# A recurrent scan's small products: values and updates stacked for contractions over 128 rows

## The chip, the cores and the metric

The kernel runs on one core of one Trainium2 chip. The metric is the device time of one execution in microseconds. The kernel is one long program, a two-part network of which the part looked at here takes about 8%.

## The reference

The reference is a network of attention, convolution, MLP and recurrent mixers. The change touches one recurrent mixer, RWKV7, over 256 context and 512 latent tokens, 8 heads of 64 channels, once forwards and once backwards:

```python
def _rwkv7_scan(S0, r, w, k, v, kk, a):
    def step(S, inp):
        r_t, w_t, k_t, v_t, kk_t, a_t = inp
        sa = jnp.einsum('bhvk,bhk->bhv', S, kk_t)
        S = (S * w_t[:, :, None, :] - sa[..., None] * (kk_t * a_t)[:, :, None, :]
             + v_t[..., None] * k_t[:, :, None, :])
        return S, jnp.einsum('bhvk,bhk->bhv', S, r_t)
    xs = tuple(jnp.swapaxes(t, 0, 1) for t in (r, w, k, v, kk, a))
    S, ys = lax.scan(step, S0, xs)
    return jnp.swapaxes(ys, 0, 1), S
...
    yf_c, Sf_c = _rwkv7_scan(S0, r_c, wf_c, k_c, v_c, kk_c, a_c)
    yb_c, Sb_c = _rwkv7_scan(S0, *_flip_seq(r_c, wb_c, k_c, v_c, kk_c, a_c))
    yf_l, _ = _rwkv7_scan(Sf_c, r_l, wf_l, k_l, v_l, kk_l, a_l)
    yb_l, _ = _rwkv7_scan(Sb_c, *_flip_seq(r_l, wb_l, k_l, v_l, kk_l, a_l))
```

Per token and head, the state S is decayed, corrected by a rank-one update (u, from S and kk) and by another (from v and k), and read by r.

## The kernel before

`rwkv_scan` (L3022 to L3332) works in chunks of 64 tokens: 12 turns (4 of context, 8 of latents) for each of two directions. A direction is an object `t` (a `Dir`) with four PSUM banks `a`, `b`, `c`, `d`. The 8 heads lie as 4 pairs q; of a pair, head h=0 has partitions 0 to 63 and head h=1 partitions 64 to 127 (`HALVES`). Almost every product is 64 rows by 64 columns by 64, in one quarter of TensorE's array: which rows and which columns follows from the partition half of the operands and of the output. The generator `heads` yields the eight (q, h).

A turn's steps are, by name, on three engines (list `order`, L3081):

- `cross` and `join` (PE) multiply decayed keys, values' keys and queries into scores of 64 x 64 and 64 x 128, which DVE (`start`, `mask`) takes to SBUF. `turn` (PE) transposes keys, `token_major` (ACT) copies them.
- `apply`, `keep`, `grow_by`, `merge` for l = 1 to 5 invert a triangular matrix by doubling: `apply` multiplies (into `d`), `keep` (DVE, L3318 and L3319) copies the wanted part into `yl[l]` under a mask, `grow_by` multiplies it into `c` and `d`, `merge` (ACT, L3259, L3262) copies the result. After l = 5 it is `solution`.
- In `apply` of the turn after, the tail of the turn before is done: l = 1 makes g = scores x v + kr x state (into `c`), `g` (ACT, L3265) copies it; l = 2 makes u = solution x g, and also starts the state's bank `a` with keys x v and the output's bank `b` with v x scores; `u` (ACT, L3268) copies u.
- `push` (PE) adds keys x u to `a` and state x queries to `b`; `state` (DVE, L3323, L3326) adds `a` to the state and decays it; `apply` with l = 3 adds u x scores to `b`, and `y` (ACT, L3271) copies `b` out. `apply` with l = 3 also turns the values of the turn to come token-major (product with an identity), `v` (ACT, L3251) copies them into `v_tok`.

So u lies on the *other* half of the partitions than its head's v, since `solution` x g is written across.

Each engine runs this list in its own program order, fully unrolled; forwards and backwards alternate, the backward direction half a list (`lag`) behind. The list is the same before and after. An engine that waits for a semaphore holds all that comes behind it in its queue. There is no DMA in the loop but that of the program's own code.

Below, a half-turn is the work between `apply` 2 of one direction and `apply` 2 of the other: one direction's second half of the list and the other's first half. There are 24 of them. In each PE goes through: apply 2 F, apply 4 B, grow_by 4 B, join B, grow_by 2 F, apply 5 B, push F, grow_by 5 B, apply 3 F, turn B, apply 1 B, grow_by 3 F, grow_by 1 B, cross F (F and B for the directions, which change places in the next).

All PE products of the loop but `turn` are recorded at L3115, the helper `one`; `turn` at L3229.

Of the kernel before, what the change touches and what calls it, by code (L numbers as in the profile page):

```python
# [13 lines left out]
ACT = mybir.ActivationFunctionType  # L14
# [3007 lines left out]
def rwkv_scan(kit, f, cum, kk, b_neg, y_out, decays, small, spare):  # L3022
# [27 lines left out]
        t.first, t.zx = take(2, 4), take(2, 4)  # L3050
        t.kb_tok = [take(2, 4) for _ in range(2)]
    for d, t in enumerate(dirs):
        t.v_tok = [take(4) for _ in range(2)]
        t.yl = [None] + [take(4) for _ in range(5)]
        t.solution, t.grow, t.state, t.g0, t.u = (take(4) for _ in range(5))
        t.fwd = d == 0
        t.decay = decays[:, d]
        t.own = t.decay[:, :, 1:65] if t.fwd else t.decay[:, :, 0:64]
        t.before = t.decay[:, :, 0:64] if t.fwd else t.decay[:, :, 1:65]
        t.bearer, t.first_bearer = small[:, d:d + 1], small[:, 2 + d:3 + d]  # L3060
        t.ends = [small[:, 4 + 12 * d + 4 * e:8 + 12 * d + 4 * e] for e in range(3)]
        t.seen = kit.const("seen_fwd" if t.fwd else "seen_back")
        t.merge = [kit.const(f"merge{l}")[:, 64 * d:64 * d + P].rearrange("p (m n) -> p m n", m=2).bitcast(mybir.dt.uint32)
                   for l in range(6)]
        t.cum, t.y = cum[d], y_out[d]
        t.a, t.b, t.c, t.d = (ps[:, 4 * d + n, :].rearrange("p (m q n) -> p m q n", m=2, q=4) for n in range(4))
        t.ab, t.cd = ps[:, 4 * d:4 * d + 2, :], ps[:, 4 * d + 2:4 * d + 4, :]
        t.prefilled, t.emptied = ph.sem("scan_prefilled"), ph.sem("scan_emptied")
        t.grown, t.bent, t.rest_bent = ph.sem("scan_grown"), ph.sem("scan_bent"), ph.sem("scan_rest_bent")
        t.crossed, t.joined, t.started, t.masked = (  # L3070
            ph.sem(f"scan_{s}") for s in ("crossed", "joined", "started", "masked"))
        t.turned, t.token_major, t.v_turned, t.v_copied = (
            ph.sem(f"scan_{s}") for s in ("turned", "token_major", "v_turned", "v_copied"))
        t.applied, t.kept, t.grown_by, t.merged = (
            [None] + [ph.sem(f"scan_{s}{l}") for l in range(1, 6)] for s in ("applied", "kept", "grown_by", "merged"))
        t.gathered, t.g_copied, t.solved, t.u_copied = (
            ph.sem(f"scan_{s}") for s in ("gathered", "g_copied", "solved", "u_copied"))
        t.state_made, t.added, t.decayed, t.out_made, t.y_copied = (
            ph.sem(f"scan_{s}") for s in ("state_made", "added", "decayed", "out_made", "y_copied"))
# [29 lines left out]
    with ph as block:  # L3109
        @block.tensor  # L3110
        def _(pe):
# [14 lines left out]
                    pe.wait_ge(sem, turn + 1)  # L3126

            def apply(t, l, i):
                level, tail, front = there(i), there(i - 1), there(i + 1)
                x = t.first[:, 1] if l == 1 else t.zx[:, 1]  # L3130
                scored = t.scored[i % 2]
                old, new = (i - 1) % 2, (i + 1) % 2
                old_scored = t.scored[old]
                if level and l == 1:
                    pe.wait_ge(t.started, i + 1)
                    pe.wait_ge(t.masked, i + 1)
                if level and l > 1:
                    pe.wait_ge(t.merged[l - 1], i + 1)
                if tail and l == 1:
                    pe.wait_ge(t.token_major, i)  # L3140
                    pe.wait_ge(t.v_copied, i)
                    pe.wait_ge(t.merged[5], i)
                if tail and l == 2:
                    pe.wait_ge(t.g_copied, i)
                    done(i, t.token_major)
                    if not level:
                        done(i - 2, t.added)
                        done(i - 2, t.y_copied)
                for q, h, half, other in heads():
                    if level:  # L3150
                        mm = one(t.d[half, 1, q, :], scored[other, h, q, 0:64], x[other, q, :])
                        if (q, h) == (3, 1):
                            mm.then_inc(t.applied[l], 1)
                    if tail and l == 1:
                        one(t.c[half, 1, q, :], old_scored[half, h, q, 0:64], t.v_tok[old][half, q, :], start=q == 0)
                    if tail and l == 2:
                        one(t.a[half, 0, q, :], t.kb_tok[old][half, h, q, :], t.v_tok[old][half, q, :], start=q == 0)
                    if front and l == 3:
                        at = offset(t, i + 1) + 1
                        mm = one(t.c[half, 1, q, :], f[half, RW_V + q, at:at + 64], same[half, :])  # L3160
                        if (q, h) == (3, 1):
                            mm.then_inc(t.v_turned, 1)
                if tail and l == 1:
                    done(i - 2, t.decayed)
                    if i == 1:
                        pe.wait_ge(t.emptied, 1)
                    for q, h, half, _ in heads():
                        mm = one(t.c[half, 1, q, :], t.kr[old][half, q, 0:64], t.state[half, q, :], start=False)
                    mm.then_inc(t.gathered, 1)
                if tail and l == 2:  # L3170
                    for q, h, half, other in heads():
                        mm = one(t.c[other, 1, q, :], t.solution[half, q, :], t.g0[half, q, :])
                        if (q, h) == (3, 1):
                            mm.then_inc(t.solved, 1)
                        one(t.b[half, 0, q, :], t.v_tok[old][half, q, :], old_scored[half, h, q, 64:P], start=q == 0)
                if tail and l == 3:
                    pe.wait_ge(t.state_made, i)
                    for q, h, half, other in heads():
                        mm = one(t.b[half, 0, q, :], t.u[other, q, :], old_scored[other, h, q, 64:P], start=False)
                    mm.then_inc(t.out_made, 1)  # L3180

            def grow_by(t, l, i):
                if l == 1:
# [1 line left out]
                if l == 2:  # L3185
                    done(i - 1, t.u_copied)
                if l == 3:
                    done(i + 1, t.v_copied)
                if there(i):
                    z = t.first[:, 0] if l == 1 else t.zx[:, 0]  # L3190
                    pe.wait_ge(t.kept[l], i + 1)
                    for q, h, half, other in heads():
                        mm = one(t.c[half, 0, q, :], t.yl[l][half, q, :], z[half, q, :])
                        if l < 5:
                            mm = one(t.d[other, 0, q, :], z[half, q, :], t.yl[l][half, q, :])
                    mm.then_inc(t.grown_by[l], 1)

            def step(t, name, l, i):
# [4 lines left out]
                elif name == "push" and there(i - 1):  # L3203
                    old = (i - 1) % 2
                    pe.wait_ge(t.u_copied, i)
                    for q, h, half, other in heads():
                        one(t.b[half, 0, q, :], t.state[half, q, :], t.kr[old][half, q, 64:P], start=False)
                        mm = one(t.a[half, 0, q, :], t.kb_tok[old][other, h, q, :], t.u[other, q, :], start=False)
                    mm.then_inc(t.state_made, 1)
                elif name == "cross" and there(i + 1):  # L3210
                    kr = t.kr[(i + 1) % 2]
                    pe.wait_ge(t.bent, i + 2)
# [22 lines left out]
        def _(act):  # L3235
            def step(t, name, l, i):
                if name == "grow" and there(i + 1):
# [7 lines left out]
                    else:  # L3245
                        act.activation(t.grow[:, :, 1:64], t.cum[:, :, at:at + 63], ACT.Exp, scale=DECAY)
                    act.activation(t.ends[(i + 1) % 3].unsqueeze(2), t.cum[:, :, at + 63:at + 64],
                                   ACT.Exp, scale=DECAY).then_inc(t.grown, 1)
                elif name == "v" and there(i + 1):
                    act.wait_ge(t.v_turned, i + 2)  # L3250
                    act.activation(t.v_tok[(i + 1) % 2], t.c[:, 1], ACT.Copy).then_inc(t.v_copied, 1)  # L3251
                elif name == "token_major" and there(i + 1):
                    act.wait_ge(t.turned, i + 2)
                    act.activation(t.kb_tok[(i + 1) % 2].rearrange("p h q n -> p h (q n)"), t.ab[:, :, 0:256],
# [10 lines left out]
                    act.activation(t.g0, t.c[:, 1], ACT.Copy).then_inc(t.g_copied, 1)  # L3265
                elif name == "u" and there(i - 1):
                    act.wait_ge(t.solved, i)
                    act.activation(t.u, t.c[:, 1], ACT.Copy).then_inc(t.u_copied, 1)  # L3268
                elif name == "y" and there(i - 1):
                    act.wait_ge(t.out_made, i)  # L3270
                    act.activation(t.y(offset(t, i - 1), 0 if i - 1 < first else 1), t.b[:, 0],  # L3271
# [2 lines left out]
            for t in dirs:  # L3274
# [1 line left out]
                if not t.fwd:  # L3276
                    act.activation(t.grow[:, :, 0:1], kit.const("ones")[:, 0:4].unsqueeze(2), ACT.Copy)
                act.activation(t.first.rearrange("p m q n -> p (m q) n"), over(kit.const("stack"), 8), ACT.Copy)
                for l in range(1, 6):
                    ins = act.activation(t.yl[l], over(kit.const("stack"), 4), ACT.Copy)  # L3280
                ins.then_inc(t.prefilled, 1)
            run("act", step)
# [2 lines left out]
        def _(dve):  # L3285
            def step(t, name, l, i):
# [29 lines left out]
                elif name == "keep" and there(i):  # L3316
                    dve.wait_ge(t.applied[l], i + 1)
                    dve.tensor_copy(t.bearer, kit.const("ones")[:, 0:1])  # L3318
                    dve.copy_predicated(t.yl[l], t.merge[l][:, 1:2].broadcast_to([P, 4, 64]),  # L3319
                                        t.d[:, 1]).then_inc(t.kept[l], 1)  # L3320
                elif name == "state" and there(i - 1):
                    dve.wait_ge(t.state_made, i)
                    dve.tensor_tensor(t.state, t.state, t.a[:, 0], ALU.add).then_inc(t.added, 1)  # L3323
# [1195 lines left out]
```

## Time and profile before

| | |
|---|---|
| time, median of 3 runs | 4143.73 us (4143.5 to 4147.54) |
| the profiled execution | 4154.6 us, its span 4152.8 us |
| TensorE busy over the span | 3822.4 us, 92% |
| granted TensorE clock, mean | 0.964 |
| the scan, from its first product to its last | 2290.9 to 2612.8 us |
| TensorE busy from 2290 to 2615 us | 255.73 us |
| VectorE, ScalarE busy in the same stretch | 168.46 us, 133.80 us |

PE is TensorE's matrix multiplication, PEld its weight load, DVE VectorE, ACT ScalarE. "x" counts records. A float32 product is two PE records and two PEld records, a transpose one of each. The granted clock is 1.00 at 2.4 GHz and 0.50 at 1.2 GHz.

### The profile page before, as it was taken

Reading aid. Unit: us, or ns where it says so; the run is one execution under the profiler, and the core shown is the slowest. Engines: PE = TensorE matmul, PEld = TensorE weight load, DVE = VectorE, ACT = ScalarE, POOL = GpSimd, SP = SyncE. Lnnn points to the kernel's source line nnn. Section 1 sums busy time; section 2 is a strip of 40 time slices with the busy share of each in tenths; the row PEclk is TensorE's granted clock in tenths of the full one; section 3 lists DMA queues with packets and bytes.
Section 4 is the critical chain, followed back from the end, with each engine's and each line's share of the span. In section 5 each row is a group of like instructions: output and inputs, shape, how many; then the busy total and the mean of one; then the engine's idle time right before and its main releaser. Section 6 shows DMA issues by size and latency. Waiting matters only on the chain. (4 is left out here: it accounts for less than half of the span.)

```text
span 4152.8 us, 69290 instructions
## 1 busy us (share of the span) xinstructions
PE 3822.4 (92%) x29040; PEld 3165.2 (76%) x29040; DVE 2175.9 (52%) x3667; ACT 1413.5 (34%) x2582; POOL 37.6 (1%) x49
## 2 busy tenths in 40 slices
PE   8999999999999999999898788899999998779998
PEld 6767777777767777777677677688888888668887
DVE  5676654444866554452566555543333465665444
ACT  3333532222434432232433434232222324353333
POOL 0000000000000000000000000000000000000000
PEclk9999999999999999999999999999999998889999
DMA  5341544442332444431011000222112220012322
GB/s 163 104 102 49 162 142 143 151 149 89 102 84 86 134 159 151 151 113 57 1 41 53 4 4 5 82 61 61 62 61 62 68 65 21 1 41 82 92 91 81
DMA packets 313958, 345.85 MB, mean 83 GB/s; under 512 B 23840, under 2 KB 289728, under 8 KB 307136
## 3 DMA queue, kind: packets, MB, share of 16 engines
q1 hardware_dynamic: 313664, 341.61, 26.0%
q8 instruction: 224, 3.67, 0.4%
q14 instruction: 70, 0.57, 0.0%
HBM read 318.77 MB, written 22.81 MB: 82 GB/s over the span
## 5 line engine op out<-in xcount | busy, mean ns | idle before, releaser
L290 DVE TENSOR_TENSOR weights_lo<-weight_ring,weights_hi 128x1024 fp32r<-128x1024 f32 x371 | 454.4, 1225 | 1287.7 <-ACT weights_hi L286 1287.5
L286 ACT ACTIVATE weights_hi<-weight_ring 128x1024 fp32r<-128x1024 f32 x371 | 392.5, 1058 | 1291.7 <-PE banks L337 1219.9
L337 PE MATMUL banks<-mlp_hidden_hi,weights_hi 128*128 128x512 f32 (+1 forms) x1280 | 475.9, 372 | 3.3 <-DVE mlp_hidden_lo L2524 3.3
L337 PE MATMUL banks<-mlp_hidden_hi,weights_lo 128*128 128x512 f32 (+1 forms) x1280 | 474.4, 371 | 0.0
L337 PE MATMUL banks<-mlp_hidden_lo,weights_hi 128*128 128x512 f32 (+1 forms) x1280 | 474.3, 371 | 0.0
L337 PE MATMUL banks<-normed_hi,weights_hi 128*128 128x258 f32 (+2 forms) x1328 | 446.5, 336 | 5.9 <-DVE rw_project_lo L686 2.5
L337 PE MATMUL banks<-mlp_lo,weights_hi 128*128 128x258 f32 (+2 forms) x1024 | 319.7, 312 | 2.8 <-issue 2.8
L337 PE MATMUL banks<-normed_hi,weights_lo 128*128 128x258 f32 (+1 forms) x928 | 316.1, 341 | 0.0
L337 PEld LDWEIGHTS banks<-mlp_hidden_hi,weights_hi 128*128 128x128 f32 x1280 | 240.2, 188 | 59.0 <-DVE mlp_hidden_lo L2524 8.2
L337 PEld LDWEIGHTS banks<-normed_hi,weights_hi 128*128 128x128 f32 x1328 | 257.0, 194 | 32.4 <-issue 7.1
L337 PEld LDWEIGHTS banks<-mlp_hidden_lo,weights_hi 128*128 128x128 f32 x1280 | 240.8, 188 | 44.0
L337 PEld LDWEIGHTS banks<-mlp_hidden_hi,weights_lo 128*128 128x128 f32 x1280 | 240.2, 188 | 43.3
L337 PE MATMUL banks<-mlp_x_hi,weights_hi 128*128 128x512 f32 x512 | 205.4, 401 | 11.9 <-DVE mlp_x_lo L313 8.3
L337 PEld LDWEIGHTS banks<-mlp_lo,weights_hi 128*128 128x128 f32 x1024 | 195.9, 191 | 14.5 <-issue 3.4
L337 PE MATMUL banks<-mlp_x_lo,weights_hi 128*128 128x512 f32 x512 | 203.5, 398 | 0.0
L337 PE MATMUL banks<-mlp_x_hi,weights_lo 128*128 128x512 f32 x512 | 203.5, 398 | 0.0
L337 PEld LDWEIGHTS banks<-normed_hi,weights_lo 128*128 128x128 f32 x928 | 176.9, 191 | 20.9
L1449 PE MATMUL banks<-scaled_hi,weights_hi 128*128 128x512 f32 x416 | 178.7, 430 | 10.6 <-PEq L146 7.2
L1449 PE MATMUL banks<-scaled_lo,weights_hi 128*128 128x512 f32 x416 | 168.5, 405 | 0.0
L1503 DVE SCALAR_TENSOR_TENSOR branch<-conv_in,pack,branch 128x512 f32<-128x512 f32 x240 | 168.3, 760 | 0.4
L1449 PE MATMUL banks<-scaled_hi,weights_lo 128*128 128x512 f32 x416 | 168.4, 405 | 0.0
L337 PE MATMUL banks<-mlp_hi,weights_hi 128*128 128x258 f32 (+1 forms) x512 | 146.3, 286 | 2.2 <-DVE mlp_lo L686 2.2
(638 smaller groups left out, 7861.0 us busy)
## 6 DMA issues: line engine op xcount, KB each, us to landing
weight_ring<-in_w SPq DMA_DIRECT2D x64, 1024.0 KB, 5.3
mod_chunks<-in_mod_w SPq DMA_DIRECT2D x24, 2048.0 KB, 10.4
weight_ring<-in_w_in SPq DMA_DIRECT2D x42, 1024.0 KB, 5.4
weight_ring<-in_w_up SPq DMA_DIRECT2D x32, 1024.0 KB, 5.9
weight_ring<-in_w_down SPq DMA_DIRECT2D x32, 1024.0 KB, 5.1
weight_ring<-in_w_in SPq DMA_DIRECT2D x52, 512.0 KB, 4.2
weight_ring<-in_w_out SPq DMA_DIRECT2D x16, 1024.0 KB, 5.5
gate_logits_dram<-gates_staged SPq DMA_DIRECT2D x48, 256.0 KB, 4.4
```

Source lines behind the costliest of these rows:

```text
L286: act.activation(self.w_hi[:, t % 2], self._raw(t), ACT.Copy).then_inc(self.w_rounded, 1)
L290: dve.tensor_tensor(self.w_lo[:, t % 2], self._raw(t), self.w_hi[:, t % 2].bitcast(F32), ALU.subtract)\
L337: mm = pe.matmul(bank, a[:, k, :], b[:, k, t0:t0 + w], start=(k == 0 and n == 0), stop=(k == KD - 1 and n == 2))
L1449: mm = pe.matmul(self.banks[n % 2], w[:, k, :], x[:, k, :], start=(k == 0 and m == 0), stop=(k == KD - 1 and m == 2))
L1503: op = dve.scalar_tensor_tensor(out=self.y[:, c, :], in0=src, scalar=tap, in1=self.y[:, c, :], op0=ALU.mult, op1=ALU.add)
```

## The change

`v_tok` and `u` become one tile `vu`, with a place for each head h: `vu[half, h]` holds v on the head's own half of the partitions, and u on the other half. The token-major keys `kb_tok` and the scores `scored` already have both halves for each h, so v's and u's contributions become one product over 128 rows. They are made in `push`: into `a` (output half by half), and, behind it, into `b`. The products of v alone in `apply` 2, and of u in `apply` 3, are gone; state x queries moves from `push` to `apply` 2. `v` and `u` now copy in two instructions of 64 partitions each. The values are turned one period later, in `apply` 3 of their own turn, h=0 with a transpose and h=1 with a product. `yl[5]` becomes `last`, block-diagonal over both heads; `grow_by` 5 is four products of 128 x 128, and `keep` 5 two masked copies of 64 partitions.

```diff
--- before.py
+++ after.py
@@ -3050,9 +3050,10 @@
...
     for d, t in enumerate(dirs):
-        t.v_tok = [take(4) for _ in range(2)]
-        t.yl = [None] + [take(4) for _ in range(5)]
-        t.solution, t.grow, t.state, t.g0, t.u = (take(4) for _ in range(5))
+        t.vu = take(2, 4)
+        t.yl = [None] + [take(4) for _ in range(4)]
+        t.last = take(4, 2)
+        t.solution, t.grow, t.state, t.g0 = (take(4) for _ in range(4))
         t.fwd = d == 0
...
@@ -3126,7 +3127,7 @@
...
             def apply(t, l, i):
-                level, tail, front = there(i), there(i - 1), there(i + 1)
+                level, tail = there(i), there(i - 1)
                 x = t.first[:, 1] if l == 1 else t.zx[:, 1]
...
@@ -3152,12 +3153,13 @@
...
                     if tail and l == 1:
-                        one(t.c[half, 1, q, :], old_scored[half, h, q, 0:64], t.v_tok[old][half, q, :], start=q == 0)
+                        one(t.c[half, 1, q, :], old_scored[half, h, q, 0:64], t.vu[half, h, q, :], start=q == 0)
                     if tail and l == 2:
-                        one(t.a[half, 0, q, :], t.kb_tok[old][half, h, q, :], t.v_tok[old][half, q, :], start=q == 0)
-                    if front and l == 3:
-                        at = offset(t, i + 1) + 1
-                        mm = one(t.c[half, 1, q, :], f[half, RW_V + q, at:at + 64], same[half, :])
+                        one(t.b[half, 0, q, :], t.state[half, q, :], t.kr[old][half, q, 64:P], start=q == 0)
+                    if level and l == 3:
+                        at = offset(t, i) + 1
+                        turned = (t.c[half, 1, q, :], f[half, RW_V + q, at:at + 64], same[half, :])
+                        mm = one(*turned) if h else pe.transpose(*turned)
                         if (q, h) == (3, 1):
...
@@ -3170,14 +3172,7 @@
...
                         mm = one(t.c[other, 1, q, :], t.solution[half, q, :], t.g0[half, q, :])
-                        if (q, h) == (3, 1):
-                            mm.then_inc(t.solved, 1)
-                        one(t.b[half, 0, q, :], t.v_tok[old][half, q, :], old_scored[half, h, q, 64:P], start=q == 0)
-                if tail and l == 3:
-                    pe.wait_ge(t.state_made, i)
-                    for q, h, half, other in heads():
-                        mm = one(t.b[half, 0, q, :], t.u[other, q, :], old_scored[other, h, q, 64:P], start=False)
-                    mm.then_inc(t.out_made, 1)
+                    mm.then_inc(t.solved, 1)
 
...
@@ -3185,14 +3180,15 @@
...
                 if l == 3:
-                    done(i + 1, t.v_copied)
+                    done(i, t.v_copied)
                 if there(i):
...
                     pe.wait_ge(t.kept[l], i + 1)
-                    for q, h, half, other in heads():
-                        mm = one(t.c[half, 0, q, :], t.yl[l][half, q, :], z[half, q, :])
-                        if l < 5:
-                            mm = one(t.d[other, 0, q, :], z[half, q, :], t.yl[l][half, q, :])
+                    for q, h, half, other in heads() if l < 5 else ():
+                        one(t.c[half, 0, q, :], t.yl[l][half, q, :], z[half, q, :])
+                        mm = one(t.d[other, 0, q, :], z[half, q, :], t.yl[l][half, q, :])
+                    for q in range(4 if l == 5 else 0):
+                        mm = one(t.c[:, 0, q, :], t.last[:, q].rearrange("p h n -> p (h n)"), z[:, q, :])
                     mm.then_inc(t.grown_by[l], 1)
...
@@ -3203,10 +3199,13 @@
...
                     pe.wait_ge(t.u_copied, i)
-                    for q, h, half, other in heads():
-                        one(t.b[half, 0, q, :], t.state[half, q, :], t.kr[old][half, q, 64:P], start=False)
-                        mm = one(t.a[half, 0, q, :], t.kb_tok[old][other, h, q, :], t.u[other, q, :], start=False)
+                    vu = t.vu
+                    for q, h, half, _ in heads():
+                        mm = one(t.a[half, 0, q, :], t.kb_tok[old][:, h, q, :], vu[:, h, q, :])
                     mm.then_inc(t.state_made, 1)
+                    for q, h, half, _ in heads():
+                        mm = one(t.b[half, 0, q, :], vu[:, h, q, :], t.scored[old][:, h, q, 64:P], start=False)
+                    mm.then_inc(t.out_made, 1)
                 elif name == "cross" and there(i + 1):
...
@@ -3246,9 +3245,11 @@
...
                                    ACT.Exp, scale=DECAY).then_inc(t.grown, 1)
-                elif name == "v" and there(i + 1):
-                    act.wait_ge(t.v_turned, i + 2)
-                    act.activation(t.v_tok[(i + 1) % 2], t.c[:, 1], ACT.Copy).then_inc(t.v_copied, 1)
+                elif name == "v" and there(i):
+                    act.wait_ge(t.v_turned, i + 1)
+                    for h, half in enumerate(HALVES):
+                        ins = act.activation(t.vu[half, h], t.c[half, 1], ACT.Copy)
+                    ins.then_inc(t.v_copied, 1)
                 elif name == "token_major" and there(i + 1):
...
@@ -3265,7 +3266,10 @@
...
                     act.wait_ge(t.solved, i)
-                    act.activation(t.u, t.c[:, 1], ACT.Copy).then_inc(t.u_copied, 1)
+                    for h, half in enumerate(HALVES):
+                        other = HALVES[1 - h]
+                        ins = act.activation(t.vu[other, h], t.c[other, 1], ACT.Copy)
+                    ins.then_inc(t.u_copied, 1)
                 elif name == "y" and there(i - 1):
...
@@ -3276,7 +3280,8 @@
...
                 act.activation(t.first.rearrange("p m q n -> p (m q) n"), over(kit.const("stack"), 8), ACT.Copy)
-                for l in range(1, 6):
+                act.activation(t.last.rearrange("p q h n -> p q (h n)"), over(kit.const("ident"), 4), ACT.Copy)
+                for l in range(1, 5):
                     ins = act.activation(t.yl[l], over(kit.const("stack"), 4), ACT.Copy)
...
@@ -3316,8 +3321,12 @@
...
                     dve.tensor_copy(t.bearer, kit.const("ones")[:, 0:1])
-                    dve.copy_predicated(t.yl[l], t.merge[l][:, 1:2].broadcast_to([P, 4, 64]),
-                                        t.d[:, 1]).then_inc(t.kept[l], 1)
+                    for h, half in enumerate(HALVES if l == 5 else ()):
+                        ins = dve.copy_predicated(t.last[half, :, h, :], t.merge[l][half, 1:2].broadcast_to([64, 4, 64]),
+                                                  t.d[half, 1])
+                    if l < 5:
+                        ins = dve.copy_predicated(t.yl[l], t.merge[l][:, 1:2].broadcast_to([P, 4, 64]), t.d[:, 1])
+                    ins.then_inc(t.kept[l], 1)
                 elif name == "state" and there(i - 1):
...
                     dve.tensor_tensor(t.state, t.state, t.a[:, 0], ALU.add).then_inc(t.added, 1)
```

## Rows read from the trace of the kernel before

**Rows 1.** The page: the engines' busy time over the whole run.

```profile
PE 3822.4 (92%) x29040; PEld 3165.2 (76%) x29040; DVE 2175.9 (52%) x3667; ACT 1413.5 (34%) x2582; POOL 37.6 (1%) x49
```

**Rows 2.** Stretches of the scan (start:end us, length, busy and records by engine, clock, DMA).

```profile
2324.80:2592.82 268.02, 218.07 (x8856) 195.68 (x8857) 143.12 (x414) 110.72 (x269) 0.00 (x0) 0.97 0.02 4
2333.04:2610.39 277.35, 224.49 (x9128) 201.58 (x9131) 141.53 (x414) 113.31 (x274) 0.00 (x0) 0.98 0.02 4
...
2387.09:2402.07 14.98, 12.48 (x424) 11.43 (x425) 6.98 (x21) 5.33 (x13) 0.00 (x0) 0.77 0.02 4
2428.23:2443.09 14.86, 12.61 (x425) 11.53 (x425) 6.95 (x21) 5.34 (x13) 0.00 (x0) 0.77 0.02 3
```

**Rows 3.** DMA queues from 2333.04 to 2610.39: packets, MB, share.

```profile
q8 instruction: 72, 1.18, 1.9%
```

**Rows 4.** Waits from 2290 to 2615: total us, times, longest.

```profile
PEld banks L3115 <- issue: 40.8, 53, 3.8
```

**Rows 5.** Timeline of PE: start, length, instruction, idle before and releaser.

```profile
2336.98 0.29 PE L3115 MATMUL banks<-weight_ring 64*64 64x64 f32 x4 [1.16 <-issue]
...
2352.34 0.21 PE L3115 MATMUL banks<-weight_ring,mixed 64*64 64x64 f32 x1 [1.17 <-issue]
```

**Rows 6.** Three stretches between such places, columns as in rows 2.

```profile
2348.48:2352.34 3.86, 2.45 (x128) 2.17 (x128) 1.30 (x4) 1.11 (x2) 0.00 (x0) 1.00 0.02 4
2352.34:2356.51 4.17, 3.56 (x126) 3.23 (x128) 2.20 (x5) 1.98 (x6) 0.00 (x0) 1.00 0.02 4
2356.51:2359.66 3.15, 2.97 (x140) 2.70 (x133) 2.92 (x10) 1.11 (x3) 0.00 (x0) 1.00 0.03 5
```

**Rows 7.** Steps of a half-turn, columns as rows 2; sum of thirteen.

```profile
2374.99:2375.94 0.95, 0.95 (x78) 0.95 (x71) 0.68 (x2) 0.00 (x0) 0.00 (x0) 1.00 0.09 17
...
2353.74:2354.37 0.63, 0.63 (x33) 0.56 (x33) 0.54 (x2) 0.06 (x1) 0.00 (x0) 1.00 0.00 0
2354.37:2355.46 1.09, 1.09 (x22) 0.97 (x17) 0.22 (x1) 0.60 (x1) 0.00 (x0) 1.00 0.00 0
2355.46:2355.98 0.52, 0.52 (x34) 0.52 (x34) 0.40 (x1) 0.00 (x0) 0.00 (x0) 1.00 0.00 0
...
2356.35:2357.27 0.92, 0.74 (x43) 0.61 (x39) 0.92 (x4) 0.47 (x1) 0.00 (x0) 1.00 0.09 18
2357.27:2357.67 0.40, 0.40 (x15) 0.40 (x18) 0.37 (x2) 0.00 (x0) 0.00 (x0) 1.00 0.00 0
2357.67:2358.74 1.07, 1.07 (x58) 1.00 (x54) 1.07 (x4) 0.38 (x1) 0.00 (x0) 1.00 0.00 0
...
2359.14:2360.17 1.03, 1.03 (x51) 1.03 (x48) 0.61 (x3) 0.92 (x3) 0.00 (x0) 1.00 0.00 0
...
sum 9.80, PE 8.76 PEld 7.92 DVE 5.81 ACT 5.41 POOL 0.00; mean PE 0.67 PEld 0.61 DVE 0.45 ACT 0.42 POOL 0.00
```

**Rows 8.** Timeline of DVE in that half-turn: keep 5, then state.

```profile
2356.78 0.43 DVE L3319 COPY_PREDICATED x<-consts,banks 128x256 f32<-128x256 uint32 x1
2357.16 0.42 DVE L3323 TENSOR_TENSOR x<-x,banks 128x256 f32<-128x256 f32 x1
```

**Rows 9.** Timeline of ACT in that half-turn: u, v, y.

```profile
2352.70 0.38 ACT L3268 ACTIVATE x<-banks 128x256 f32<-128x256 f32 x1 [2.74 <-PE banks L3115]
...
2359.74 0.38 ACT L3251 ACTIVATE mixed<-banks 128x256 f32<-128x256 f32 x1
2360.01 0.39 ACT L3271 ACTIVATE mixed<-banks 128x256 f32<-128x256 f32 x1
```

**Rows 10.** Timeline of PE: join and turn (rows*columns of array, operand).

```profile
2354.37 1.16 PE L3115 MATMUL banks<-weight_ring 64*128 64x128 f32 x16
...
2358.74 0.46 PE L3229 MATMUL banks<-consts,weight_ring 64*128 64x64 f32 x8
```

**Rows 11.** Timeline of PE elsewhere in the program, two bursts over 128 rows.

```profile
1292.59 1.89 PE L1569 MATMUL banks<-projected,weight_ring 128*128 128x64 f32 x16
...
2284.04 3.26 PE L3014 MATMUL banks<-consts,stat 128*64 128x128 f32 x54
```

## The prediction

> **What bounds the kernel now.** The page says TensorE [rows 1], 92% of the span; the scan is about 322 of 4153 us. I went through it in this order: stretches of the scan, for the length of a half-turn; the waits, for what PE waits for; the timeline of PE, for where; and single steps, for what the work would take without that.
>
> From 2324.80 to 2592.82 there are 21 half-turns, 12.76 us each. Two of them, 14.98 and 14.86 us, ran with a clock of 0.77 on the mean, that is, for a part at 1.2 instead of 2.4 GHz [rows 2]. The other 19 take (268.02 - 29.84) / 19 = **12.54 us**.
>
> The longest entry of PE's waits is not another engine but "issue", no cause that the trace shows: 40.8 us in 53 places [rows 4]. They lie in the middle of steps: 1.16 us in cross, where only one wait stands at the top, 1.17 us eight products from the end of apply 2 [rows 5]. And they are evenly spaced. Between 2333.04 and 2610.39 there are 9128 matmul and 9131 load records, and exactly 72 packets in the queue that carries instructions, 16 KB each [rows 2, 3]. That is 253.6 records per packet, 256 with some 2.4 semaphore instructions that the busy counts leave out. The stretch between two such places holds 128 + 128 records in 3.86 us [rows 6]. So code for PE arrives in blocks of 256 instructions, and a block takes about 3.8 us to come. A half-turn has 424 products' records, as many loads [rows 2], and 8 waits: 856 instructions, 3.34 blocks; 12.54 / 3.34 = **3.75 us a block**. A stretch that was not held up ran in 3.15 us [rows 6]: PE itself could go faster than its code.
>
> The Trainium skill says otherwise (Runtime: NRT & Kernel Launch, Instruction fetch mechanics): the cost of crossing such a boundary is mostly hidden. This trace disagrees, with over a microsecond at a boundary [rows 5]. By the rule PE's work alone would count.
>
> PE's work alone: thirteen undisturbed steps sum to 9.80 us and apply 2 takes 0.95 [rows 7]: **10.75 us** a half-turn, waits for other engines included. The time now is set by code (12.54), not by work (10.75).
>
> **The change, part by part**, per half-turn.
>
> *Records.* In the pairing of matmul records: apply 2 falls from 64 to 48 (state x queries replaces keys x v, v x scores goes), apply 3 from 48 to 28 (16 for u x scores; four transposes have one record each where a product has two, as turn has 8 for 8 and join 16 for 8 [rows 10]), grow_by 5 from 16 to 8; push stays at 32. That is 44 fewer, and 44 fewer loads: 856 becomes 768, 3.00 blocks. By code alone: 3.00 x 3.75 = **11.25 us**.
>
> *push.* Products of 64 x 64 run in four quarters at once: grow_by's 32 records take 0.52 us, eight rounds of 0.06 [rows 7]. Over 128 rows two column halves are left, so 32 records are sixteen rounds. That two halves do run side by side is seen elsewhere: 54 records 128*64 with 128 columns in 3.26 us, 0.11 a pair [rows 11], which is 0.12 a pair with the last one's own length in it, as join's pairs take 0.11 for the same width (its step of 1.09 us, less 0.20 for what follows below, over 8). So push grows by 8 x 0.06 = 0.47. A change of array shape costs too: before join, grow_by takes 0.63 instead of 0.52, and join 1.09 instead of 0.89, 0.31 for two changes, 0.15 each [rows 7]. But push is followed by idle PE: its step of 0.92 is 0.52 of work and then the wait for the other direction's keep 5, which ends at 2357.21 [rows 7, 8]. keep 5 becomes two copies of half the partitions; between nothing and a second one at DVE's pace, 2357.16 - 2356.78 = 0.38 [rows 8]. I take 0.38, since the elements per partition stay. push then lasts the longer of 0.52 + 0.47 + 0.15 = 1.14 and 0.92 + 0.38 = 1.30: **+0.38**. The order holds state back behind keep 5 as before; DVE is busy 143 of 268 us [rows 2].
>
> *grow_by 5.* Four products of full 128 x 128 with 64 columns are 8 records. Such a burst takes 1.89 us for 16, the last one's own length in it [rows 11]: 0.11 a record, 0.90 for eight, against 0.40 [rows 7]; one more change of shape behind it: **+0.65**.
>
> *apply 3.* Eight rounds fewer: **-0.47**. Its transposes lie among products; bounds: free, or a change of shape around each (a rival below). I take free, because the array's 64*64 shape stays.
>
> *apply 2.* Both parts had a partner in the other quarters; the rounds stay: 0.
>
> *v and u.* Each copy becomes two, +0.28 on ACT (start to start of the v and y copies, 0.27 [rows 9]; bound 0 if half the partitions were half the time). u is hidden: the copy begins at 2352.70 and grow_by 2, its first reader, at 2355.46 [rows 7, 9], behind apply 4, grow_by 4 and join; without them it would cost its 0.28. v isn't: ACT does token_major, v, y and g in a row, and grow_by 3 starts at 2360.17, where v's copy ends at 2360.12 [rows 7, 9]: **+0.28**. y's product is now ready a step earlier, but its copy stands behind v's: nothing.
>
> *Once.* One wider prefill, 0.2 us a direction: nothing. The order list is the same; no DMA is added.
>
> *Sum.* 10.75 + 0.38 + 0.65 - 0.47 + 0.28 = **11.6 us** of work against 11.25 of code. The work is no lighter than before, it is heavier by 0.84; what gets lighter is the code. Two limits so near each other: work now leads, and where it is dense (apply 1, grow_by 3, grow_by 1, cross, apply 2) some stall stays. Between 0 and 1.25 (nothing absorbed); I take 0.25, because the block that was not held up, from 2356.51, came right behind one that PE had spent 4.17 us on [rows 6]: a slow block lets the next one's code come in time. So 11.85 against 12.54, 0.69 x 24 half-turns = 16.6 us. The profiled execution of 4154.6 us would be 4138; it lies 10.9 above the median of the runs, and from 4143.7 the forecast is **4127 us**.
>
> **Rivals.**
>
> *Code decides alone (0.18).* The added work falls into time in which PE now waits: 11.25, 1.29 x 24 = 31 us less: 4113. For it: before, PE's waits for others cost nothing beside the stalls. Against it: 11.6 of work has little left to absorb.
>
> *The column halves of push take turns (0.13).* 64-column records of two halves in 0.11 a pair instead of 0.06: +0.9, less some slack in push, so 12.4 to 12.5: **no change**, 4142. [Rows 11] don't exclude it: at 128 columns a pair's two weight loads of 64 columns could take turns and still fit. The Trainium skill has a rule that would do this (TensorE: Matmul & The Clock Gate, Part 3): weight loads overlap running products only where the rows of the array differ, and over 128 rows they never do.
>
> *The transposes of apply 3 empty the array (0.10), slower.* Four transposes among 24 records of products are eight changes at 0.15 each: +1.2, so 13.05, 0.51 x 24 = 12 us more: 4156. It decides from 0.69 / 8 = 0.09 us a change. For it: every seen change of shape costs 0.15. Against it: turn's eight transposes run at the products' pace, 0.46 us for the eight [rows 10].
>
> *The change doesn't thin the stalls (0.04), slower.* If the 1.8 us a half-turn (12.54 - 10.75) had a cause other than the count of instructions, 11.6 + 1.8 = 13.4, 20 us more: 4164. Against it: 72 packets for 72 x 256 instructions.
>
> **How the numbers follow.** The likeliest case has 0.47; 0.08 is for small sums around zero or beyond. The half-clock stretches add doubt: each cost 2.4 us (14.9 - 12.5) [rows 2], and I can't tell from these rows what will bring one; there may be none or two more. Low end: code alone, no such stretch, 4109; high end: halves in turns and one more, 4147. A measurement can tell about 0.2%, 8.3 us. Faster: 0.47 + 0.18 + a part of the rest, 0.69. Within: 0.13 + 0.03 = 0.16. Slower: 0.10 + 0.04 + 0.01 = 0.15.
>
> **What would show it.** In the changed kernel: about 8 instruction packets fewer in the scan, still one per 256 instructions; half-turns near 11.85 us; "issue" far below 40.8 us; more waiting of PE for keep 5 and v; grow_by 5 at 0.9 us; push at sixteen rounds. Wrong, if push takes 1.7 us of work, if gaps stand around the transposes, or if half-turns stay at 12.5 with stalls as long as now.

## The result, and the profile after

The changed kernel takes 4179.9 us (median of 4 runs, 4178.65 to 4181.02) against 4145.56 for the one before (median of 4): ratio 1.0082, interval 1.0071 to 1.0094. It is 34 us (0.8%) **slower**; 4127 was forecast, between 4109 and 4147.

The page of the kernel after, to be set beside [rows 1], and the packets of instructions in the 21 half-turns between the first and the last apply 2 (70 of them before):

```profile
PE 3883.9 (93%) x27984; PEld 3215.3 (77%) x27984; DVE 2189.5 (52%) x3691; ACT 1434.8 (34%) x2630; POOL 37.1 (1%) x49
...
q8 instruction: 63, 1.03, 1.5%
```

TensorE has 1056 matmul records fewer, as counted, and is busy 61 us longer. Seven packets fewer there, and still one for every 256 instructions: that sign of the prediction came true. The 21 half-turns (compare [rows 2]), one undisturbed, one with a fall of the clock, and the stretch right behind such a fall:

```profile
2334.31:2619.03 284.72, 262.97 (x7955) 230.17 (x7949) 155.94 (x436) 129.13 (x312) 0.00 (x0) 0.94 0.02 4
2360.78:2373.94 13.16, 12.03 (x380) 10.36 (x380) 7.52 (x22) 6.14 (x15) 0.00 (x0) 1.00 0.02 4
2400.27:2414.24 13.97, 13.09 (x380) 11.62 (x380) 7.51 (x22) 6.25 (x15) 0.00 (x0) 0.88 0.02 4
2409.80:2413.20 3.40, 3.40 (x114) 3.28 (x112) 0.84 (x3) 2.29 (x6) 0.00 (x0) 0.50 0.02 5
```

An undisturbed half-turn is 13.17 us where it was 12.54, and eleven times it is between 13.15 and 13.17: nothing random holds PE up any more. The code stalls are gone; the wait for no cause that the trace shows ("issue"), which was 40.8 us [rows 4], is

```profile
PEld banks L3116 <- issue: 3.1, 4, 1.2
```

Where the time went shows in the steps of one half-turn, apply 5, push, grow_by 5, apply 3, and (behind turn) apply 1 (compare [rows 7]):

```profile
2365.24:2365.81 0.57, 0.57 (x29) 0.50 (x21) 0.57 (x1) 0.33 (x1) 0.00 (x0) 1.00 0.00 0
2365.81:2366.99 1.18, 1.15 (x35) 1.01 (x33) 1.14 (x5) 0.27 (x1) 0.00 (x0) 1.00 0.00 0
2366.99:2368.03 1.04, 1.04 (x9) 0.97 (x9) 1.01 (x3) 0.00 (x0) 0.00 (x0) 1.00 0.08 16
2368.03:2370.04 2.01, 2.01 (x29) 1.41 (x28) 0.82 (x3) 0.38 (x1) 0.00 (x0) 1.00 0.00 0
...
2370.43:2371.85 1.42, 1.17 (x53) 1.03 (x49) 0.72 (x3) 1.27 (x4) 0.00 (x0) 1.00 0.00 0
```

apply 3, which should have fallen from 1.07 to about 0.6 us, takes 2.01 for 28 records. PE's timeline inside it; L3162 is the transpose:

```profile
2368.28 0.24 PE L3162 MATMUL banks<-consts,rw_features 64*64 64x64 f32 x1
2368.45 0.27 PE L3116 MATMUL banks<-weight_ring 64*64 64x64 f32 x1
...
2368.57 0.22 PE L3116 MATMUL banks<-weight_ring 64*64 64x64 f32 x1
2368.72 0.24 PE L3162 MATMUL banks<-consts,rw_features 64*64 64x64 f32 x1
2368.90 0.27 PE L3116 MATMUL banks<-weight_ring 64*64 64x64 f32 x1
```

From the last product's start to the transpose is 0.15 us (2368.57 to 2368.72), from there to the next product 0.17 to 0.18, where rounds of products follow at 0.06. There are four transposes a half-turn, all of one form, and wherever the clock is full both gaps are the same each time (75 transposes: 0.15 before, 0.17 to 0.18 behind). The rows show these gaps; what the array does in them they don't show. The prediction and the expectations call it emptying the array.

By place, in the profiled executions (26.4 us apart): the 21 half-turns 284.72 - 268.02 = 16.7 us; the stretch ahead of them 9.5 (they begin at 2334.3, not 2324.8). It runs at a lower clock, and its first turns have spread transposes too; how the 9.5 us divide between the two isn't shown. Here it is in the kernel after and then in the one before:

```profile
2290.30:2334.30 44.00, 30.44 (x664) 26.65 (x664) 18.21 (x50) 17.54 (x44) 0.00 (x0) 0.62 0.01 2
```

```profile
2290.30:2324.80 34.50, 21.98 (x713) 19.25 (x713) 18.16 (x52) 17.05 (x45) 0.00 (x0) 0.80 0.01 3
```

and 0.2 in all other places. The medians are 34 apart: before's profiled execution lay 9 us above its median, after's 1 us.

### The profile page after: what moved, and what is told of

Read it like the earlier page. It is cut to its first block and busy times, and to the rows that moved or that the text cites. A ratio compares the mean times of both kernels' runs of the same rounds, so it can differ in the third digit from the quotient of the medians.

```text
span 4179.2 us, 67250 instructions
## 1 busy us (share of the span) xinstructions
PE 3883.9 (93%) x27984; PEld 3215.3 (77%) x27984; DVE 2189.5 (52%) x3691; ACT 1434.8 (34%) x2630; POOL 37.1 (1%) x49
```

## The experiments

Theory A is the prediction's account with its third rival in place of "free": code comes at 3.75 us per 256 instructions, PE's own work is a second limit, and each change between product and transpose costs a gap. The rivals stand in the expectations.

**1. The whole change without transposes** (`e1_products_only`).

```diff
-                        mm = one(*turned) if h else pe.transpose(*turned)
+                        mm = one(*turned)
```

> The changed kernel with the four transposes per turn and direction (values of h=0) made as products again, all else as changed. Theory A (the transposes empty the array: 0.15 us in front of and 0.17 us behind each, and code comes in blocks of 256 instructions at 3.75 us): apply 3 falls from 2.02 to about 0.6 us, a half-turn from 13.17 to between 11.8 and 12.1 us (776 instructions are 11.4 us of code), the clock stays at 2.4 GHz in most of the loop, and the time falls to 4128 to 4142 us, at or under the kernel before. Rival B (contractions over 128 rows and their changes of shape are what costs): apply 3 shrinks little or its time comes back in push and grow_by 5, the time stays above 4160 us.

Measured: 4134.9 us, ratio to before 0.9974 (0.9964 to 0.9985). The 21 half-turns:

```profile
2327.44:2578.05 250.61, 225.13 (x8032) 200.58 (x8032) 154.05 (x435) 128.21 (x312) 0.00 (x0) 1.00 0.02 4
```

11.93 us each, 11.77 where no stall for code is left; the clock stays up in them. One line turns a loss of 34 us into a gain of 11: theory A, and four transposes a half-turn cost 45 us.

**2. Only the transposes, in the kernel before** (`e2_transposes_only`): the same edit the other way round.

> The kernel before with only the values' h=0 products replaced by transposes. Theory A: apply 3 grows by 1.4 us, work per half-turn from 10.75 to 12.2 us, code 848 instructions or 12.4 us; both near each other, so half-turns of 12.5 to 13.0 us and 0 to 15 us more in the time, more if the clock falls behind the emptied stretch as it did in the changed kernel. If transposes among products are free: 8 instructions fewer, 3 us less.

Measured: 4150.7 us, ratio 1.0008 (0.9999 to 1.0018). Half-turns and the wait for code:

```profile
2328.94:2595.28 266.34, 237.07 (x8776) 207.09 (x8777) 144.77 (x414) 111.31 (x269) 0.00 (x0) 0.99 0.02 4
```

```profile
PEld banks L3115 <- issue: 15.1, 26, 1.2
```

apply 3 grew from 1.07 to 2.38 us in the median, the half-turn only from 12.54 to 12.68. The wait "issue" fell from 40.8 to 15.1: while PE stood in these gaps, code arrived. The clock fell once in the 21 half-turns, for 3.4 us. The same transposes cost next to nothing in the old kernel (the interval ends at 0.2%, 7 us) and 45 us in the new one. A part tried alone under one limit says little of what it costs under another.

**3. The stacking alone** (`e3_stack_alone`): as 1, and `yl[5]`, keep 5 and grow_by 5 as before.

```diff
...
-                    for q, h, half, other in heads() if l < 5 else ():
-                        one(t.c[half, 0, q, :], t.yl[l][half, q, :], z[half, q, :])
-                        mm = one(t.d[other, 0, q, :], z[half, q, :], t.yl[l][half, q, :])
-                    for q in range(4 if l == 5 else 0):
-                        mm = one(t.c[:, 0, q, :], t.last[:, q].rearrange("p h n -> p (h n)"), z[:, q, :])
+                    for q, h, half, other in heads():
+                        mm = one(t.c[half, 0, q, :], t.yl[l][half, q, :], z[half, q, :])
+                        if l < 5:
+                            mm = one(t.d[other, 0, q, :], z[half, q, :], t.yl[l][half, q, :])
...
```

> The changed kernel without transposes and with keep 5 and grow_by 5 as before: only the stacking of values and updates. Theory A: work falls against e1 by about 0.6 (grow_by 5) and 0.3 (second masked copy) to 10.9 us a half-turn, code is 792 instructions or 11.6 us, so 11.6 to 11.8 us a half-turn and 4122 to 4132 us: faster than before by code alone. If code is not what limits the kernel before, it comes out at 4145 us or above, since the work is not lighter than before.

Measured: 4130.7 us, ratio 0.9962 (0.9949 to 0.9975). 245.51 / 21 = 11.69 us a half-turn, "issue" 15.4 us: code limits again, 792 instructions at 3.78 us a block. The block-diagonal last product saves 16 instructions and costs 0.6 us of work. By the medians on the same chip it loses 4 us, though the intervals of 1 and 3 overlap.

**4. More instructions, no more rounds** (`e4_dummy_records`, on the kernel before).

```diff
+                    if level and l > 3:
+                        one(t.c[half, 1, q, :], scored[half, h, q, 0:64], x[half, q, :])
```

> The kernel before with eight more products in apply 4 and eight in apply 5, in the two quarters of the array that these steps leave free, into a place that nobody reads before it is overwritten (no result changes). 32 more matmul records and 32 loads a half-turn, no more rounds. If code limits (3.75 us per 256 instructions): 920 instructions, +0.94 us a half-turn, +20 to +23 us in all. If the array's rounds or the waits limit: +0 to +3 us.

Measured: 4169.9 us, 24 more than before (ratio 1.0055, 1.0042 to 1.0068; 20 to 23 were expected). 281.07 / 21 = 13.38 us for 3.59 blocks, 3.72 us a block, three short falls of the clock included; "issue" 59.5 us. Records in idle quarters of the array, at no cost there, cost their code. How much a block more costs is less sure: the medians give 24 / 24 / 0.25 = 4.0 us, but the two profiled executions lie only (281.07 - 268.02) / 21 = 0.62 us a half-turn apart, 2.5 us a block. Between runs 3 and 4, half a block apart, it is 3.3 us by the medians and 3.4 by the traces.

**5. The transposes in a row** (`e5_grouped_transposes`, on the changed kernel).

```diff
...
+                if level and l == 3:
+                    for q in range(4):
+                        mm = pe.transpose(t.c[0:64, 1, q, :], f[0:64, RW_V + q, at:at + 64], same[0:64, :])
+                    mm.then_inc(t.v_turned, 1)
```

(in place of those in the loop over heads, which keeps the products of h=1)

> The changed kernel with its four transposes in a row behind the products of apply 3 instead of one after every third product. Theory A1 (what costs is each change between product and transpose): two changes for eight, apply 3 about 1.0 us instead of 2.02, half-turns near 12.2 us, no falls of the clock in the loop, time 4140 to 4150 us. Rival A2 (each transpose costs by itself, wherever it stands, about 0.3 us): apply 3 stays near 1.9 us and the time near 4178 us.

Measured: 4136.3 us, ratio 0.9969 (0.9959 to 0.9979), 44 us less than with the same four transposes spread out. Half-turns of 251.34 / 21 = 11.97 us:

```profile
2328.80:2580.14 251.34, 227.07 (x7948) 203.28 (x7948) 154.10 (x435) 128.40 (x312) 0.00 (x0) 1.00 0.02 4
```

From apply 3's first record to its last transpose it is 0.81 us. PE's timeline at its end, where L3165 is the grouped transposes and L3230 is turn:

```profile
2372.43 0.22 PE L3116 MATMUL banks<-consts,rw_features 64*64 64x64 f32 x1
2372.58 0.30 PE L3165 MATMUL banks<-consts,rw_features 64*64 64x64 f32 x2
2372.67 0.27 PE L3230 MATMUL banks<-consts,weight_ring 64*128 64x64 f32 x1
2372.72 0.27 PE L3165 MATMUL banks<-consts,rw_features 64*64 64x64 f32 x2
```

Behind the last product the first transpose stands 0.15 us later. The others follow without such a gap, and turn's, of another shape, run in among them. What costs is the change, and rival A2, a price of each transpose wherever it stands, is out. The time is better than expected (4140 to 4150, half-turns near 12.2): two changes were priced, and one is there, which takes the place of the one ahead of turn. The four transposes, one behind the other, aren't free: apply 3 and turn together take 1.21 us (2371.96 to 2373.17) for 1.02 in run 1, and the half-turn 11.97 for 11.77.

**6. The dummy products in the changed kernel** (`e6_changed_dummy`): the lines of 4.

> The changed kernel with the same dummy products as in the run on the kernel before (8 in apply 4, 8 in apply 5, free quarters of the array): 832 instructions a half-turn instead of 768, 12.2 us of code against 13.2 us of work. If the limit has moved from code to work: 0 to +3 us against the changed kernel, where the kernel before took +24. If code still set the pace: +20 us or more, above 4198 us.

Measured: 4179.6 us, against 4179.9 without. The 21 half-turns:

```profile
2332.96:2617.48 284.52, 261.29 (x8627) 226.57 (x8621) 156.03 (x436) 128.88 (x312) 0.00 (x0) 0.96 0.02 4
```

The instructions that cost 24 us in the kernel before cost nothing here on balance: the limit has moved from code to work. But the balance hides two things. The clock fell 6 times in these half-turns, not 10, which at 0.8 us each gives back 3 us; and some stalls for code are back: 284.52 - 21 x 13.17 - 6 x 0.8 = 3 us. So the 16 added products cost some 3 us, an eighth of what they cost before. Why the clock fell less often isn't shown.

**7, 8. v's copies earlier** (`e7_stack_early_v` on 3, `e8_products_early_v` on 1), by one place in the list (the expectation says two):

```diff
-("pe", "apply", 3), ("dve", "keep", 3), ("act", "v", 0), ("act", "y", 0),
+("pe", "apply", 3), ("act", "v", 0), ("dve", "keep", 3), ("act", "y", 0),
```

> The stacking alone (no transposes, grow_by 5 as before), with the v copy two places earlier in the order list, so that on ACT it comes ahead of the other direction's token_major. The two v copies then lie beside turn and apply 1: apply 1's step falls from 1.41 to 1.04 us again, work from 10.9 to 10.6 us. Code stays at 11.6 us a half-turn, so if that limits, 0 to 4 us less than 4130.7; if work limited it, 9 us less.

> The whole change but for the transposes, with the v copy earlier in the order as well. Work 11.77 - 0.37 = 11.4 us a half-turn, code (776 instructions) 11.4 us: half-turns of 11.5 to 11.7 us, 3 to 8 us less than 4134.9. If v's second copy were not what lengthened apply 1's step, no change.

Measured: 4127.5 us (ratio 0.9952, 0.9938 to 0.9966) and 4129.5 us (0.9959, 0.9945 to 0.9972). apply 1's step fell to 0.93 us in both, grow_by 3's grew from 0.68 to 0.83. The half-turns are 11.68 and 11.72 us, against 11.69 and 11.93 without. So v's copies were on the path in 1, and were covered by code in 3. On another chip the first of the two gave

> The same kernel as the run before (stacking alone, v early), for a comparison on the same chip: 4124 to 4131 us.

and 4132.9 us (0.9965, 0.9953 to 0.9977), outside what was expected, so that its lead over 3 isn't shown.

**9. Both limits lowered** (`e9_stack_grouped`): 7 with the grouped transposes of 5.

> The stacking alone with v early, and four of the eight values' products as transposes in a row behind the others: 784 instructions a half-turn for 792, 11.5 us of code, and some 0.2 us more of work, 10.8 us. Code limits, so work is covered: 1 to 5 us less than 4127.5. If work limited it, 4 to 5 us more.

Measured: 4126.7 us, ratio 0.9949 (0.9935 to 0.9962), with half-turns of 11.48 us for 3.06 blocks: 3.75 us a block. It ran beside the repeated kernel of 7 and came out 6 us below it. Their intervals overlap a little, so a gain isn't shown; it has the lowest median and ratio of all.

## Why the prediction was wrong

*What bounds the kernel before: right.* Code did, at the price read from the trace. Run 4 added 0.25 blocks a half-turn and cost 24 us, 20 to 23 expected; run 6 showed the same instructions at some 3 us once code no longer bound.

*The step that failed: "I take free, because the array's 64*64 shape stays".* The transposes weren't free. Two rows spoke for it: turn's eight transposes at the products' pace, which stand in a row, and the unchanged shape. Neither shows a transpose next to a product. The eight changes cost 2.01 - 0.63 = 1.4 us a half-turn (0.63 is apply 3 in run 1), 0.17 each. That is the third rival, which priced them at 0.15 and got 10%; its break-even of 0.09 us was half of what was measured. So a term was put at nothing that is 1.4 us, and it turned the sign of the forecast.

*That rival's own sum was too small*: 4156 for 4180. It had 13.05 us for a half-turn, 13.17 measured, and that is in part luck: it took 11.6 of work without the changes (11.77 measured), 1.2 for them (1.40) and 0.25 of stalls (none left). It did not have the clock. In the changed kernel it fell to half ten times within the 21 half-turns, each time 0.05 to 0.42 us behind turn's first record, that is right behind apply 3, and each fall cost 13.97 - 13.17 = 0.8 us; the stretch ahead ran at 0.62 instead of 0.80. In the half-turns of runs 1 and 5 there was none, and their stretches ahead ran at 0.73. From run 1 to the changed kernel the half-turns of the profiled executions grew by 284.72 - 250.61 = 34 us: 8 are the falls, and 21 x 1.24 = 26 the longer half-turns (1.40 of changes, less 0.16 of stalls in run 1 that they cover). The stretch ahead adds 2334.3 - 2327.4 = 7. The medians differ by 45; where the other 4 lie isn't shown.

*All the rest of the sum, as run 1 shows it* (terms in us a half-turn, forecast and measured as steps' medians): push and what goes into it 0.38, and 0.46 (push 0.91 to 1.17, apply 5 in front 0.37 to 0.57, the change of shape); its rounds were paired: PE went through 32 records over 128 rows in a step of 1.18 us, where halves in turns needed 1.7 of work by the prediction. So the rival in which column halves take turns is out. The Trainium skill's rule beside it (TensorE: Matmul & The Clock Gate, Part 3), that a weight load overlaps running products only where the rows differ, doesn't hold in this step. grow_by 5 0.65, and 0.62. apply 3 -0.47, and -0.44. v +0.28, and +0.37: each copy of 64 partitions takes as long as one of 128, and the two don't overlap (two copies of 128 in a row start 0.27 apart [rows 9]),

```profile
2371.04 0.76 ACT L3251 ACTIVATE mixed<-banks 64x256 f32<-64x256 f32 x2
```

against 0.38 for one of 128 [rows 9]. keep 5's second masked copy cost 0.47, not 0.38:

```profile
2366.04 0.90 DVE L3325 COPY_PREDICATED x<-consts,banks 64x256 f32<-64x256 uint32 x2
```

Together work came to 11.77 where 11.6 was forecast, and the half-turn with what is left of the stalls to 11.93 where 11.85 was. Without the transposes the account gives 4127; run 1 took 4135. Of these 8 us, 0.08 x 24 = 2 are the half-turns and 2.6 the stretch ahead, which began its first full half-turn at 2327.4 and not 2324.8; where the rest lies isn't shown.

*The rule that crossing a block of code is mostly hidden* (the Trainium skill, Runtime: NRT & Kernel Launch, Instruction fetch mechanics) does not hold for this loop: the kernels that code limits take 3.7 to 3.8 us per 256 instructions, where PE would be faster, and run 4 shows that instructions alone make the time longer. In the changed kernel, at 4.4 us of work a block (13.17 / 3.00), it does hold, but for the 3 us of run 6.

Open: what makes the clock fall. Behind the spread transposes it fell 10 times in the changed kernel and 6 in run 6, but only once in run 2, where the loop had stalls besides. And it fell without them, at other places of the half-turn: twice in the kernel before, for 6.8 us each [rows 2], three times in run 4 and once in run 7. So the spread transposes bring falls in a dense loop; no run says which part of the loop's activity decides it.

## What to carry to other kernels

Look for idle time that recurs every 256 instructions of one engine: there the count of instructions is the price, idle quarters of the array are not free, and extra work is hidden until the stalls are used up. A change that lowers one limit uncovers what that limit hid, so cost each part against the new limit, with its own timeline row for every neighbourhood it makes: a transpose beside a transpose said nothing of one beside a product. Put operations of one kind in a row.

## What the runs showed of the hardware

- In a run of float32 products of 64 x 64 in the array's quarters (0.06 us a round), a transpose of the same shape starts 0.15 us behind the last product, and the next product 0.17 us behind it (the kernel after); in a row, transposes follow at 0.06 to 0.09 us (run 5).
- Code for TensorE came at 3.72 to 3.78 us per 256 instructions, as a mean over the scan, in four kernels of 784 to 920 instructions a half-turn (before, runs 3, 4 and 9).
- Within the 21 half-turns the clock fell to half right behind apply 3 ten times with the transposes spread, and not at all with the same four in a row (run 5). In the kernel before, whose half-turns had stalls, spread transposes brought one fall (run 2).
- A ScalarE copy of 64x256 from PSUM took 0.38 us, as long as one of 128x256; two masked VectorE copies of 64x256 in a row took 0.90 us, one of 128x256 0.43.
